# Four groups of value rows summed on TensorE, and the forgetting heads' scores made in pairs, in an encoder block whose last part gathers rows

## The chip, the cores and the metric

One core of a Trainium2 chip runs the whole program. The metric is the device time in microseconds, the median of the runs. It has five engines with a queue each, run in program order and tied by semaphores: TensorE (matmuls), VectorE, ScalarE, GpSimd (which here issues the gathers) and SyncE (which issues the plain loads); and 16 DMA engines that all transfers share.

## The reference, cut to what matters

The block works on 512 tokens of 1024 numbers (4 tiles of 128 tokens). It has an attention part and a PEER part:

```python
h = h + mixed @ w_out                 # mixed: 8 forgetting heads and 4 differential heads
hn = _rmsnorm(h, norm2_g)
# PEER, for each token and each of 8 heads: two top-16 searches over 128 key scores,
# a top 16 over the 16x16 sums, then
u_sel = jnp.take(u_tab, eidx, axis=0)          # 16 rows of 1024 from 16384
hid = gelu(einsum('thkd,td->thk', u_sel, xb)) * g
v_sel = jnp.take(v_tab, eidx, axis=0)          # 16 rows of 1024
h = h + einsum('thk,thkd->td', hid, v_sel)
out = _rmsnorm(h, final_g)
```

All of it is float32. The scores of a forgetting head are q times k, with 64 numbers contracted, plus a bias from the running sum of the log forget gates, for keys up to the token's tile: 128, 256, 384 or 512 columns for tiles 0 to 3.

## The kernel before, in words

**The order of the work.** Tile 0 is taken through attention first (`BEFORE`). Then its PEER heads start while tiles 1 to 3 are still to go through attention. Seven PEER heads of tile 0 (`HOST_HEADS`) host that other work: this is the hosted loop. The remaining 25 head turns (one of tile 0, eight of each other tile) follow in the tail, in which a gather brings a `u` row and a `v` row in one go (`peer_uv`, 8 KB per token), VectorE makes the dot products, ScalarE a diagonal of the coefficients, and TensorE sums the `v` rows in two banks (`peer_group`, L994).

**The hosted loop.** A head has 16 rows per token, taken in 4 groups (`GRP`) of 4 (`COLS`), so there are 28 slots, one for each group. A slot has nine gaps. In gaps 0, 2, 4 and 6 VectorE makes a dot product of the slot's own group (`dot`, L1541), in gaps 1, 3, 5 and 7 it adds one value row of the group two slots earlier (`BEHIND = 2`): `h[tile 0] += coef * v_row` (`add_row`, L1577, one 128x1024 instruction). The coefficients (`coefs`, L1567) come in gap 1 from a gelu that ScalarE makes in gap 4 of the slot before. In between stand the pieces of the next head's top-k search. What is called T0 later is the end of the last addition of a group.

**The pieces.** What is left of tiles 1 to 3 is cut into pieces. Each has a cost (`share`), and the pieces are laid over the first 27 slots in proportion to their cumulated cost:

```python
for p in later:
    k = int(at / total * (SLOTS - 1) * GAPS)
    ...
    AFTER[k].append(p)
    at += share(p)
```

`total` is 551.2. Every engine runs the pieces of a gap in that order. The kinds are: `project` (a slab of the input weights: 8 matmuls of 384 columns at L786, or of 256 at L778 for values), `attend` (one step, below), `mix`, `mixT`, `outproj` (4 matmuls of 512 columns, L860, added into `h` by VectorE, L1414), `hT`, `query` and `keys`.

**An attend step.** The forgetting heads of tiles 1, 2 and 3 are steps 0 to 23 of one run (8 heads for each tile). In step s TensorE makes the scores of head s (q times k at L929, the bias at L933, both on the same half of the rows: partitions 0 to 63 for even heads, 64 to 127 for odd ones), then transposes the probabilities of head s - 3 (L950) and multiplies those of head s - 4 with the values (L972). Scores go to a ring of three banks (`sc_b`). VectorE's part of step s takes the scores through the mask with a running minimum (L1442); ScalarE takes the exponential (L1195) and the copy of the transpose (L1188). At step 27 (the last head's values) VectorE scales the mixed values (L1450, L1453). The differential heads follow as steps of their own, with two maps in each, matmuls of the two row halves side by side.

**The product banks.** Each piece that ends in a bank has a number in the list `MM`; it uses bank number modulo 3 of `mm0`, `mm1`, `acc0`, and TensorE waits until the piece three earlier has been emptied (`mm_bank`).

**The rings.** `u_ring` and `v_ring` hold four rows each. GpSimd issues alternately the gather of a `u` row four ahead (L685) and of a `v` row (L692):

```python
def gather_v(n, c):
    if n or c >= V_RING:
        pool.wait_ge(added, TOPK * n + c + 1 - V_RING)
```

so the `v` row c of a group can only be fetched when the row c of the group before has been added.

## Time and profile before

| | |
|---|---|
| median of 3 runs | 1542.28 us (1540.99 to 1546.88) |
| profiled execution, its own time | 1541.62 us |
| its span in the trace | 1539.8 us |
| TensorE busy | 1269.3 us (82%) |
| VectorE busy | 1077.6 us (70%) |
| ScalarE busy | 459.8 us (30%) |
| GpSimd busy | 751.5 us (49%) |
| DMA | 596.50 MB, mean 387 GB/s |
| mean granted TensorE clock | 0.939 |

The busy shares are means over stages with different limits, so they are to be read by stretch: in the rows of the next section but one, each stretch has the busy time of the engines in it, the granted clock and the DMA engines' busy share. A busy TensorE counts overlapping matmuls once; each float32 matmul appears as two rows (passes). The L numbers are lines of the kernel printed above.

### The profile page before, as it was taken

Reading aid. Unit: us, or ns where it says so; the run is one execution under the profiler, and the core shown is the slowest. Engines: PE = TensorE matmul, PEld = TensorE weight load, DVE = VectorE, ACT = ScalarE, POOL = GpSimd, SP = SyncE. Lnnn points to the kernel's source line nnn. Section 1 sums busy time; section 2 is a strip of 40 time slices with the busy share of each in tenths; the row PEclk is TensorE's granted clock in tenths of the full one; section 3 lists DMA queues with packets and bytes.
Section 4 is the critical chain, followed back from the end, with each engine's and each line's share of the span. In section 5 each row is a group of like instructions: output and inputs, shape, how many; then the busy total and the mean of one; then the engine's idle time right before and its main releaser. Section 6 shows DMA issues by size and latency. Waiting matters only on the chain.

```text
span 1539.8 us, 13062 instructions
## 1 busy us (share of the span) xinstructions
PE 1269.3 (82%) x3727; PEld 658.2 (43%) x3727; DVE 1077.6 (70%) x2520; ACT 459.8 (30%) x1200; POOL 751.5 (49%) x637
## 2 busy tenths in 40 slices
PE   9999999988888488999787777677886787777778
PEld 7766655665545234444333333233332233332333
DVE  3247699999988867566666676666666766666654
ACT  3432355466343022222222222221222222222212
POOL 0016477675667443454544554445444554444440
PEclk9999999999989699999899999989999999999998
DMA  9669799997999999999999999999999999999995
GB/s 382 250 250 413 275 330 351 370 376 268 340 371 392 391 421 416 421 421 421 421 422 422 421 422 421 421 422 421 422 421 421 422 422 421 422 420 422 421 421 208
DMA packets 99741, 596.50 MB, mean 387 GB/s; under 512 B 11480, under 2 KB 11480, under 8 KB 42328
## 3 DMA queue, kind: packets, MB, share of 16 engines
q0 software_dynamic: 89856, 536.91, 86.0%
q1 hardware_dynamic: 9816, 58.77, 9.6%
q8 instruction: 31, 0.51, 0.1%
q14 instruction: 38, 0.31, 0.0%
HBM read 593.54 MB, written 2.10 MB: 387 GB/s over the span
## 4 chain that ended last, share of the span: by engine, by line
DMA 42%; PE 15%; DVE 6%; POOL 3%; issue 2%; ACT 2%; DVEq 0%; POOLq 0%
PE acc L994 13%; DMA map_mem<-in_peer_uv_dram,eidx 10%; DMA w_ring<-in_peer_uv_dram,eidx 9%; DMA v_all<-in_peer_uv_dram,eidx 7%; DMA act_mem<-in_peer_uv_dram,eidx 6%; DMA v_ring<-in_peer_uv_dram,eidx 3%; DMA mix_mem<-in_peer_uv_dram,eidx 3%; DMA u_ring<-in_peer_uv_dram,eidx 3%; DMA v_ring<-in_peer_v_dram,eidx 2%; PE mm L786 1%; ACT diag L1228 1%; DVE map_mem L1549 1%; DVE w_ring L1549 1%; PE sc L786 1%; POOL v_ring L692 1%
## 5 line engine op out<-in xcount | busy, mean ns | idle before, releaser
L1220 ACT ACTIVATE gel<-hid 128x4 f32<-128x4 f32 x126 | 25.8, 205 | 722.2 <-DVE hid L1549 712.5
L685 POOL DMA_INDIRECT u_ring<-in_peer_u_dram,eidx x112 | 136.8, 1221 | 172.9 <-DVE eidx L1529 99.5
L994 PE MATMUL acc<-v_all,diag 128*128 128x512 f32 x256 | 129.2, 651 | 61.1 <-ACT diag L1228 60.6
L692 POOL DMA_INDIRECT v_ring<-in_peer_v_dram,eidx x112 | 133.4, 1192 | 66.4 <-DVE h L1577 38.0
L1577 DVE SCALAR_TENSOR_TENSOR h<-v_ring,coef,h 128x1024 f32<-128x1024 f32 x112 | 143.9, 1284 | 14.3 <-DMA v_ring<-in_peer_v_dram,eidx 11.3
L994 PE MATMUL acc<-map_mem,diag 128*128 128x512 f32 x248 | 123.3, 644 | 32.0 <-ACT diag L1228 32.0
L994 PE MATMUL acc<-v_ring,diag 128*128 128x512 f32 x248 | 120.1, 629 | 32.3 <-ACT diag L1228 28.7
L1541 DVE CUSTOM_DVE_ANT_0 u_ring<-u_ring,hn 128x1024 f32<-128x1024 f32 x112 | 136.6, 1220 | 14.2 <-DMA u_ring<-in_peer_u_dram,eidx 14.0
L994 PE MATMUL acc<-u_ring,diag 128*128 128x512 f32 x248 | 119.1, 626 | 27.4 <-ACT diag L1228 25.8
L1228 ACT ACTIVATE diag<-ident,coef 128x128 f32<-128x128 f32 x392 | 126.3, 390 | 39.1 <-DVE coef L1567 30.8
L711 POOL DMA_INDIRECT v_all<-in_peer_uv_dram,eidx x64 | 76.1, 1189 | 92.3 <-PE acc L994 81.7
L711 POOL DMA_INDIRECT map_mem<-in_peer_uv_dram,eidx x62 | 73.8, 1190 | 95.1 <-PE acc L994 87.0
L711 POOL DMA_INDIRECT v_ring<-in_peer_uv_dram,eidx x62 | 77.2, 1246 | 79.0 <-PE acc L994 68.2
L994 PE MATMUL acc<-w_ring,diag 128*128 128x512 f32 x176 | 89.2, 655 | 24.5 <-ACT diag L1228 24.4
L1549 DVE CUSTOM_DVE_ANT_0 v_all<-v_all,hn 128x1024 f32<-128x1024 f32 x62 | 75.4, 1225 | 47.9 <-DMA v_all<-in_peer_uv_dram,eidx 47.9
L994 PEld LDWEIGHTS acc<-v_all,diag 128*128 128x128 f32 x256 | 51.9, 209 | 132.0 <-issue 132.0
L786 PE MATMUL mm<-act_mem,w_ring 128*128 128x384 f32 x304 | 104.0, 497 | 3.0 <-ACT act_mem L1118 3.0
L1549 DVE CUSTOM_DVE_ANT_0 map_mem<-map_mem,hn 128x1024 f32<-128x1024 f32 x62 | 75.3, 1224 | 43.5 <-DMA map_mem<-in_peer_uv_dram,eidx 43.5
L994 PE MATMUL acc<-act_mem,diag 128*128 128x512 f32 x176 | 86.0, 634 | 23.3 <-ACT diag L1228 23.3
L711 POOL DMA_INDIRECT u_ring<-in_peer_uv_dram,eidx x62 | 72.0, 1161 | 66.7 <-PE acc L994 59.4
L1549 DVE CUSTOM_DVE_ANT_0 v_ring<-v_ring,hn 128x1024 f32<-128x1024 f32 x60 | 72.9, 1226 | 44.1 <-DMA v_ring<-in_peer_uv_dram,eidx 44.1
L1549 DVE CUSTOM_DVE_ANT_0 u_ring<-u_ring,hn 128x1024 f32<-128x1024 f32 x60 | 72.8, 1224 | 41.4 <-DMA u_ring<-in_peer_uv_dram,eidx 41.4
(281 smaller groups left out, 2331.9 us busy)
## 6 DMA issues: line engine op xcount, KB each, us to landing
w_ring<-in_slabs_dram SPq DMA_DIRECT2D x29, 1024.0 KB, 8.4
v_ring<-in_slabs_dram SPq DMA_DIRECT2D x6, 1024.0 KB, 11.2
u_ring<-in_slabs_dram SPq DMA_DIRECT2D x6, 1024.0 KB, 10.9
map_mem<-in_slabs_dram SPq DMA_DIRECT2D x6, 1024.0 KB, 7.9
h<-in_x_dram SPq DMA_DIRECT2D x4, 512.0 KB, 12.5
u_ring<-in_peer_u_dram,eidx POOLq DMA_INDIRECT x112, 6.9
v_ring<-in_peer_v_dram,eidx POOLq DMA_INDIRECT x112, 7.1
v_all<-in_x_cols_dram SPq DMA_DIRECT2D x3, 512.0 KB, 7.4
```

The costliest lines, as they stand in the source:

```text
L685: nc.gpsimd.indirect_dma_start(out=u_ring[:, c % U_RING, :], out_offset=None, in_=peer_u[0], in_offset=bass.IndirectOffsetOnAxis(ap=eidx[n ...
L692: nc.gpsimd.indirect_dma_start(out=v_ring[:, c % V_RING, :], out_offset=None, in_=peer_v[0], in_offset=bass.IndirectOffsetOnAxis(ap=eidx[n ...
L711: nc.gpsimd.indirect_dma_start(out=row_mem[place], out_offset=None, in_=peer_uv, in_offset=bass.IndirectOffsetOnAxis(ap=eidx[n % 3][:, c:c ...
L786: last = nc.tensor.matmul(bk[:, 0:n], w[:, c, q * P:(q + 1) * P], actT[:, c, 0:n], start=(c == 0), stop=(c == KC - 1))
L994: last = nc.tensor.matmul(acc[half][:, :], diag[:, c % COLS, :], v_row(n, c)[:, half * BANK:(half + 1) * BANK], start=first, stop=(n % PH ...
L1220: nc.scalar.activation(gel[:, par, g0:g0 + COLS], hid[:, par, g0:g0 + COLS], ACT.Gelu).then_inc(gelu_done, 1)
L1228: nc.scalar.activation(diag[:, c, :], ident[:, :], ACT.Copy, scale=coef[:, par, g0 + c:g0 + c + 1]).then_inc(diag_done, 1)
L1541: nc.vector.tensor_tensor_reduce(out=u_ring[:, c % U_RING, :], in0=u_ring[:, c % U_RING, :], in1=hn[:, :], scale=1.0, scalar=0.0, op0=ALU. ...
L1549: nc.vector.tensor_tensor_reduce(out=u_row(n, c), in0=u_row(n, c), in1=hn[:, :], scale=1.0, scalar=0.0, op0=ALU.mult, op1=ALU.add, accum_o ...
L1577: nc.vector.scalar_tensor_tensor(out=ht, in0=v_ring[:, c % V_RING, :], scalar=coef[:, par, c:c + 1], in1=ht, op0=ALU.mult, op1=ALU.add).th ...
```

## The change

Two things are changed.

1. The value rows of four groups of tile 0 (5, 9, 13 and 17, of 28) are no longer added by VectorE. A new piece `sum` stands in gap 0 of slot k + 2, ahead of the other pieces of the slot, with a share of 10 each in the placement (the total becomes 591.2, so the pieces behind move by a few gaps). In it ScalarE makes four diagonals of the coefficients (128x128), and TensorE multiplies the four rows with them, in two halves of 512 columns, into two of the three product banks. VectorE adds the two banks into `h` in gap 1 of the next slot (or ahead of an `outproj` that comes first). The coefficients of such a group are made in gap 0 instead of gap 1. A `v` place is given back when TensorE has read it. The diagonals lie in memory that `z_f` and `e_f` used on 8 partitions.
2. The scores of the forgetting heads are made for two heads at a time: in every even step the two products q times k, then the two biases; odd steps make none.

In the diff the places come in this order: the placement, the list of banks, the give-back of rows, GpSimd's gather, TensorE's piece and its scores, ScalarE's piece, VectorE's piece, its addition of the sums, and its hosted loop.

```diff
 BEHIND = 2
+SUMMED = (5, 9, 13, 17)
+SHARE_SUM = 10.0
...
     total, at = sum(share(p) for p in later), 0.0
+    total += SHARE_SUM * len(SUMMED)
+    summed_at = {(k + BEHIND) * GAPS: ("sum", k) for k in SUMMED}
     for p in later:
         k = int(at / total * (SLOTS - 1) * GAPS)
+        while summed_at and k >= min(summed_at):
+            slot = min(summed_at)
+            AFTER[slot].append(summed_at.pop(slot))
+            at += SHARE_SUM
+            k = int(at / total * (SLOTS - 1) * GAPS)
...
+        elif kind == "sum":
+            MM += [(*p, half) for half in range(2)]
...
+        def row_taken(i):
+            if i // COLS in SUMMED and i % COLS == COLS - 1:
+                return mm_full, mm_done(("sum", i // COLS, 1))
+            return added, i + 1 - sum(COLS * k + COLS - 1 <= i for k in SUMMED)
...
             def gather_v(n, c):
                 if n or c >= V_RING:
-                    pool.wait_ge(added, TOPK * n + c + 1 - V_RING)
+                    pool.wait_ge(*row_taken(TOPK * n + c - V_RING))
...
                     last.then_inc(mm_full, 1)
+                elif kind == "sum":
+                    k, = p
+                    pe.wait_ge(*row_taken(COLS * k - 1))
+                    banks = [mm_bank((kind, k, half)) for half in range(2)]
+                    for c in range(COLS):
+                        pe.wait_ge(v_in[c % V_RING], 16 * (k * COLS // V_RING + 1))
+                        pe.wait_ge(sum_diag_done, COLS * SUMMED.index(k) + c + 1)
+                        for half in range(2):
+                            last = nc.tensor.matmul(banks[half][:, :], sum_diag[:, c, :], v_ring[:, c % V_RING, half * BANK:(half + 1) * BANK],
+                                                    start=(c == 0), stop=(c == COLS - 1))
+                            if c == COLS - 1:
+                                last.then_inc(mm_full, 1)
+                        if c < COLS - 1:
+                            last.then_inc(added, 1)
...
+            def pair_scores(g, step):
+                t, first = at_step(g, 0, step)
+                nk, j = P * (t + 1), GROUPS[g].index(t)
+                if first == 0:
+                    pe.wait_ge(selq_ready, 2 * (t + 1))
+                both = [(HD * (m % 2), m // 2, map_no[(t, m)]) for m in (first, first + 1)]
+                for lo, ch, k in both:
+                    if k >= len(sc_b):
+                        pe.wait_ge(sc_drained, k + 1 - len(sc_b))
+                    nc.tensor.matmul(sc_b[k % len(sc_b)][:, 0:nk], qT[lo:lo + HD, ch, j * P:(j + 1) * P], kv_t[lo:lo + HD, ch, 0:nk],
+                                     start=True, stop=False)
+                for lo, ch, k in both:
+                    nc.tensor.matmul(sc_b[k % len(sc_b)][:, 0:nk], selq[lo:lo + 40, ch, t % 2, :], caug[lo:lo + 40, 0:nk],
+                                     start=False, stop=True).then_inc(sc_full, 1)
+
             def scores(g, half, step):
-                if at_step(g, half, step):
+                if half == 0:
+                    if step % 2 == 0 and at_step(g, half, step):
+                        pair_scores(g, step)
+                elif at_step(g, half, step):
...
                                              scale=rstd2[:, t:t + 1]).then_inc(mm_copied, 1)
+                elif kind == "sum":
+                    n, par, g0 = group_at(p[0])
+                    act.wait_ge(coef_done, p[0] + 1)
...
+                    for c in range(COLS):
+                        nc.scalar.activation(sum_diag[:, c, :], ident[:, :], ACT.Copy,
+                                             scale=coef[:, par, g0 + c:g0 + c + 1]).then_inc(sum_diag_done, 1)
...
                 elif kind == "outproj":
                     g, sl, t = p
+                    if sums_due:
+                        add_sum(sums_due.pop())
...
+            def add_sum(k):
+                for half in range(2):
+                    bk = mm_wait(("sum", k, half))
+                    hs = h[:, 0, half * BANK:(half + 1) * BANK]
+                    nc.vector.tensor_tensor(out=hs, in0=bk[:, :], in1=hs, op=ALU.add).then_inc(mm_drained, 1)
...
                     behind = group_at(k - BEHIND)
                     for gap in range(GAPS):
                         c = gap // 2
+                        if gap == 0 and k - BEHIND in SUMMED:
+                            coefs(*behind)
+                            sums_due.append(k - BEHIND)
+                        if gap == 1 and k - BEHIND - 1 in SUMMED and sums_due:
+                            add_sum(sums_due.pop())
...
-                        elif gap < GAPS - 1 and k >= BEHIND:
+                        elif gap < GAPS - 1 and k >= BEHIND and k - BEHIND not in SUMMED:
```

Three more waits on `added` (of the combined gathers, of `eidx` and of the last part) and the wait in `add_row` are written with `row_taken` in the same way; ahead of a row that follows a summed group, `add_row` waits until the banks of the sum have been added.

## Rows read from the trace of the kernel before

**Rows 1.** Stretches: us, busy us (instructions) of PE, PEld, DVE, ACT, POOL; clock, DMA share, GB/s

```profile
225.00:265.00 40.00, 38.67 (x151) 23.41 (x150) 39.62 (x89) 21.96 (x46) 29.45 (x25) 0.96 0.96 357
265.00:327.00 62.00, 61.29 (x286) 43.02 (x285) 59.27 (x113) 28.29 (x55) 45.51 (x38) 1.00 0.98 370
327.00:400.00 73.00, 62.38 (x318) 42.44 (x318) 70.57 (x159) 50.66 (x135) 49.78 (x41) 0.91 0.88 320
400.00:490.00 90.00, 77.67 (x245) 43.34 (x244) 81.79 (x160) 25.12 (x63) 62.14 (x53) 0.92 0.95 362
500.00:800.00 300.00, 247.76 (x606) 115.86 (x607) 204.32 (x486) 73.32 (x194) 142.06 (x124) 0.91 1.01 417
```

**Rows 2.** Timeline of VectorE: start us, duration us, instruction, idle before it

```profile
214.02 1.27 DVE L1577 SCALAR_TENSOR_TENSOR h<-v_ring,coef,h 128x1024 f32<-128x1024 f32 x1
215.56 1.21 DVE L1541 CUSTOM_DVE_ANT_0 u_ring<-u_ring,hn 128x1024 f32<-128x1024 f32 x1
...
266.54 1.31 DVE L1577 SCALAR_TENSOR_TENSOR h<-v_ring,coef,h 128x1024 f32<-128x1024 f32 x1
...
269.22 1.28 DVE L1577 SCALAR_TENSOR_TENSOR h<-v_ring,coef,h 128x1024 f32<-128x1024 f32 x1
270.42 0.68 DVE L1442 CUSTOM_DVE_ANT_0 map_mem<-sc,act_mem 128x512 f32<-128x512 f32 x1
...
318.37 1.31 DVE L1577 SCALAR_TENSOR_TENSOR h<-v_ring,coef,h 128x1024 f32<-128x1024 f32 x1
...
379.94 1.27 DVE L1577 SCALAR_TENSOR_TENSOR h<-v_ring,coef,h 128x1024 f32<-128x1024 f32 x1
...
391.42 0.68 DVE L1414 TENSOR_TENSOR h<-mm,h 128x512 f32<-128x512 f32 x1
...
454.49 0.22 DVE L1567 SCALAR_TENSOR_TENSOR coef<-gel,gate_inv,gexp 128x4 f32<-128x4 f32 x1 [4.83 <-ACT gel L1220]
```

**Rows 3.** Timeline of TensorE, neighbouring passes of one kind merged

```profile
194.52 0.48 PE L929 MATMUL sc<-store 64*128 64x256 f32 x1 [0.47 <-ACT v_all L1082]
194.53 0.48 PE L929 MATMUL acc<-store 64*128 64x256 f32 x1
...
195.49 0.59 PE L929 MATMUL sc<-store 64*128 64x256 f32 x2
...
208.28 0.70 PE L929 MATMUL acc<-store 64*128 64x256 f32 x2
...
209.34 0.44 PE L950 MATMUL tr<-ident,map_mem 128*128 128x128 f32 x2
...
267.55 1.12 PE L929 MATMUL sc<-store 64*128 64x512 f32 x2
...
269.47 0.55 PE L950 MATMUL tr<-ident,map_mem 128*128 128x128 f32 x3
...
323.04 3.67 PE L778 MATMUL acc<-w_ring,act_mem 128*128 128x256 f32 x16
326.55 1.00 PE L972 MATMUL o<-v_all,map_mem 128*128 128x64 f32 x8
...
368.47 2.07 PE L929 MATMUL acc<-store 64*128 64x512 f32 x2 [5.34 <-DVE negmax L1442]
```

**Rows 4.** Groups of ScalarE by line and shape: busy us, mean ns

```profile
L1228 ACT ACTIVATE diag<-ident,coef 128x128 f32<-128x128 f32 x392 | 126.3, 390 | 39.1 <-DVE coef L1567 30.8 <-PE acc L994 8.3
```

**Rows 5.** The chain that ended last, in the tail: start us, us

```profile
596.87 13.73 PE acc L994 x32
```

**Rows 6.** Timeline of GpSimd, its gathers of value rows

```profile
216.41 1.18 POOL L692 DMA_INDIRECT v_ring<-in_peer_v_dram,eidx  x1 [0.31 <-issue]
...
270.10 1.21 POOL L692 DMA_INDIRECT v_ring<-in_peer_v_dram,eidx  x1 [0.30 <-issue]
...
323.45 1.68 POOL L692 DMA_INDIRECT v_ring<-in_peer_v_dram,eidx  x1 [0.30 <-issue]
```

**Rows 7.** The tile v_ring, 200 to 450 us: issue to landing

```profile
DMA to landing us min/median/max: 4.7/6.6/10.0
```

More of the change, by code:

```diff
@@ L387, in build @@
         c_all = sb("c_all", [FH, SEQ])
[L388 to L389 removed]
+        gate_mem = sb("gate_mem", [P, 2 * max_n])
+        z_f = gate_mem[0:FH, 0:max_n]
+        e_f = gate_mem[0:FH, max_n:2 * max_n]
+        sum_diag = gate_mem[:, 0:COLS * P].rearrange("p (a n) -> p a n", a=COLS)
         selq = mix_mem[:, D:D + FH * P].rearrange("p (a b n) -> p a b n", a=FH // 2, b=2)
@@ L923, in scores @@
                             pe.wait_ge(sc_drained, k + 1 - len(sc_b))
-                        bk = sc_b[k % len(sc_b)]
-                        if m < FH:
-                            lo, ch = HD * (m % 2), m // 2
-                        else:
-                            lo, ch = HD * ((m - FH) % 2), KC // 2 + (m - FH) // 2
-                        mo = nc.tensor.matmul(bk[:, 0:nk], qT[lo:lo + HD, ch, j * P:(j + 1) * P], kv_t[lo:lo + HD, ch, 0:nk],
-                                              start=True, stop=(m >= FH))
-                        if m < FH:
-                            mo = nc.tensor.matmul(bk[:, 0:nk], selq[lo:lo + 40, m // 2, t % 2, :], caug[lo:lo + 40, 0:nk], start=False, stop=True)
-                        mo.then_inc(sc_full, 1)
+                        lo, ch = HD * ((m - FH) % 2), KC // 2 + (m - FH) // 2
+                        nc.tensor.matmul(sc_b[k % len(sc_b)][:, 0:nk], qT[lo:lo + HD, ch, j * P:(j + 1) * P], kv_t[lo:lo + HD, ch, 0:nk],
+                                         start=True, stop=True).then_inc(sc_full, 1)
             def turned_map(g, half, step):
@@ L1573, in add_row @@
                 dve.wait_ge(coef_done, GRP * n + c // COLS + 1)
-                if n or c:
-                    dve.wait_ge(added, TOPK * n + c)
+                before = (TOPK * n + c - 1) // COLS
+                if c % COLS == 0 and before in SUMMED:
+                    dve.wait_ge(*emptied(("sum", before, 1)))
+                elif n or c:
+                    dve.wait_ge(*row_taken(TOPK * n + c - 1))
                 ht = h[:, n // PH, :]
```

14 lines of the change are left out of this document (7 added, 7 removed).

## The prediction, made before the change was run

> **What bounds the kernel now.** I read the stretch table first [rows 1]. From 500 us on the 16 DMA engines are full (share 1.01, 417 GB/s), and nothing after that frees them. From there the bytes that are left decide, and one microsecond lost or won before that point arrives at the end about one to one. What can move it is the hosted loop (28 slots of 9 gaps, about 110 to 490 us), in which VectorE works through tile 0's rows with the pieces of tiles 1 to 3 between them. There VectorE is busy 39.6 of 40 us (225 to 265 us) and 59.3 of 62 us (265 to 327 us), TensorE 38.7 and 61.3 of the same, and the DMA share is 0.96 and 0.98. So three engines are all near full up to 327 us; later TensorE (62.4 of 73 us) and DMA (0.88) have room and VectorE (70.6 of 73 us) hasn't.
>
> Then the timelines, to see who leads. TensorE finishes the scores of head step 17 (the second one of 512 columns) at 269.47, and VectorE takes them at 270.42 [rows 2, 3]. TensorE's lead is 1 us there, and VectorE doesn't wait: they are just in time. A stop of TensorE longer than its lead becomes a stop of VectorE.
>
> **VectorE's share of the change.** 16 row additions go. One lasts 1.28 us, and 1.20 us from its start to the next instruction's (269.22 to 270.42) [rows 2]: 16 x 1.20 = 19.2 us. Eight 128x512 additions from PSUM come, 0.68 us each (391.42) and, by the same overlap of 0.08, 0.6 us of the chain [rows 2]: 8 x 0.6 = 4.8 us. Net -14.4 us, 3.6 per group. ScalarE gets 16 diagonals of 0.39 us [rows 4], 6.2 us, hidden: it is busy 50.7 of 73 us at most [rows 1]. If they weren't hidden they'd stand inside the sums' wait for rows below, since four of them (1.6 us) are over before the last row lands.
>
> **TensorE's share.** A sum is 4 rows by 2 halves, 8 matmuls of 512 columns. The chain shows 32 passes of that kind in 13.73 us, two passes to a matmul: 0.86 us each [rows 5]. 8 x 0.86 = 6.9 us per sum, 27.5 us for four. The paired scores give some back. A head at 256 columns takes 1.06 us on its own (208.28 to 209.34), yet two heads whose matmuls happened to stand together went at 194.52 to 195.5, both banks at once, 0.97 us for two [rows 3]. The second of the rows at 194.5 starts 0.01 us after the first, so row halves do run side by side and the saving is real: about 1.1 us per pair at 256 columns. At 512 a head is 1.92 us (267.55 to 269.47) [rows 3] and a pair, at the 0.43 us of a 512-column pass four times and a start of 0.1, about 1.8: saving 2.0. At 384 columns, between the two, a head is 1.5 and a pair 1.4: saving 1.6. Four pairs per tile: 4 x (1.1 + 1.6 + 2.0) = 18.8 us, less one pair at 256 that is already together: 17.7 us. TensorE's work grows by 9.8 us net. The Trainium skill says in TensorEngine Tiling (Array Packing), Key Properties, that different row tiles can execute in parallel but that changing the tiling mode drains the engine; by the first half the pairing wins what the rows say, by the second a part of it would go at each switch between 128-row and 64-row work, and the switches are in both kernels, fewer in the new one.
>
> **The wait that comes with the sum.** TensorE works in program order, and the sum stands in gap 0 of slot k + 2, ahead of that slot's steps. It has to wait (a) for the last addition of group k - 1, call its end T0, and (b) for row c = 3 of its own group. That row's gather may start only when the same ring place is free, at T0, because group k - 1's last row held it. Now VectorE asks for it a whole slot later and it's there; in the new order TensorE asks at once. GpSimd is near full too: it issues it at 216.41 for group 5 (T0 = 215.3, the end of the addition at 214.02), 270.10 for group 9 (267.9) and 323.45 for group 13 (319.7) [rows 2, 6], so 1.1, 2.2 and 3.8 us late; for group 17 (381.2) I take the 1.1. From issue to landing takes 4.7 to 10.0, median 6.6 us [rows 7]. The last two matmuls take 1.7 us. The sum ends at T0 + 9.4, 10.5, 12.1 and 9.4 us.
>
> Next who is late. By the placement rule (a piece's cumulated share over the total, 551.2 before and 591.2 after, times 243 gaps) I placed the pieces of both kernels. After each sum stands something that VectorE needs in the same slot:
> - group 5, slot 7: steps 9 (gap 5) and 10 (gap 6). TensorE adds 0.8 us of transposes and values and 1.4 of the pair: ready at T0 + 11.7. VectorE, with four dots of 1.2 us [rows 2], coefficients of 0.3 and two strips of 0.5, is there at T0 + 6.1. Wait 5.6.
> - group 9, slot 11: step 18 (gap 5), the pair at 512 columns, 1.8 us: ready T0 + 12.5. VectorE after three dots: T0 + 3.9. Wait 8.6.
> - group 13, slot 15: step 27 (gap 8) needs the last values; before them stand step 26 (1.3), a value projection (3.5, from 323.04 to 326.55) and step 27's own 0.9 [rows 3]: ready T0 + 17.8, VectorE there at T0 + 5.1. Wait 12 to 13, I take 12. In the old order these values are done by 327.5, T0 + 7.8.
> - group 17, slot 19: mixT, then differential step 11 (gap 5): 0.45 + 1.8 + 1.1: ready T0 + 12.9, VectorE at T0 + 3.9. Wait 9.0.
>
> Sum of waits 35.2 us. Then the banks: a sum holds two of three product banks until gap 1 of the next slot. Only after group 17 does this bite: the two output projections of slot 20, gaps 1 and 2, can't begin before the banks are emptied; each is 4 matmuls, 3.4 us, against about 2.1 and 1.8 us of other VectorE work: 1.3 + 1.6 = 2.9 us.
>
> **Credits.** VectorE's wait of 4.83 us at slot 24 for a gelu behind a query copy [rows 2] shrinks, since that query now stands behind the gelu; it's partly taken up a slot later: 3. Tile 0's pairs at 128 columns, where TensorE leads the start: 0 to 2.4, I take 1.5.
>
> **Sum.** -14.4 + 35.2 + 2.9 - 4.5 = +19.2 us. The profiled execution took 1541.6 us by its own count (span 1539.8), 0.7 below the median of 1542.3, so I add to it, 1560.8, and say 1560.
>
> **Unknown costs, from both sides.** Landing of the last row: 4.7 to 10.0 us instead of 6.6, so -7.6 to +13.6 over four. GpSimd's lag: 1.1 to 3.8 us, -4 to +7. The pair at 384 and 512 columns, which no row shows: between the one at 256 columns scaled by columns (1.5 and 1.9 us) and no overlap at all (3.0 and 3.8 us), in which case TensorE is the bound from 225 to 327 us and 12 us more are due. The clock: after a wait of 5.34 us the two passes at 368.47 took 2.07 us where 1.12 (267.55) is usual [rows 3]: twice as long, as at the lower of its two clock levels (1.2 for 2.4 GHz); the stretch from 327 to 400 us, where this happened, has a mean granted clock of 0.91 [rows 1]. If each sum's wait has this effect, what follows it costs 1 to 3 us more each, 4 to 12 in all. The Trainium skill's page TensorE: Matmul & The Clock Gate (Why this matters for your kernels) warns of idle gaps between bursts; by the trace it does happen after such waits, but inside a sum the rows come one by one, so I count nothing for it in the sum.
>
> **Rivals.**
> - *The additions' saving passes on (faster).* If the last row lands early and the paired scores have put TensorE ahead, VectorE is not stopped and 14.4 us come out of its chain. What decides is the wait per sum: below 3.6 us each it is a gain. For it: rows can land in 4.7 us, and odd steps need no scores. Against: even 1.1 + 4.7 + 1.7 us is T0 + 7.5, ahead of which no step of the slot can be scored. DMA caps it as well: 0.96, 0.98, 0.88 and 0.95 of four stretches [rows 1] leave about 16 us in all but 1.2 between 265 and 327 us. Time 1528 to 1534.
> - *Break-even.* Waits of 4 to 6 us a sum, as group 5's: four times 5.6 is 22.4, with 2.9 - 14.4 - 4.5: +6.4, time 1548; with fast landings (1.9 each) 1540.
> - *TensorE becomes the bound.* The stalls and low clock together, or no overlap of the pairs: +30 to +40, 1572 to 1582.
> - *Nothing reaches the end* because the DMA tail absorbs it: against it stands that the tail is full from 500 us [rows 1], with no idle to give.
>
> **How the numbers follow.** Stalls as worked out 0.50, TensorE as the bound 0.10, break-even 0.20, saving passes on 0.18, tail absorbs 0.02. A difference below 0.5% (7.7 us, 1534.6 to 1550.0) is about what a measurement of this kernel can't tell from none. The likeliest has 1552 to 1573 by itself; with break-even and part of the gain on one side and part of the bound case on the other, 1532 to 1578. Faster 0.20, same 0.20, slower 0.60.
>
> **What would show it.** In the new profile: TensorE waiting 4 to 8 us at the sum's line on v_ring landings, four times; VectorE's strip line waiting for the score matmuls at about 225, 280, 335 and 400 us, the third longest (at the mix of slot 15); slot 20's output additions waiting for their matmul; score rows of two banks that start within 0.02 us of each other; the full-rate DMA stretch beginning some 15 to 20 us later. I am wrong if VectorE stays above 95% busy through slots 7, 11, 15 and 19, or if TensorE's lead at a sum turns out to be many microseconds because pairs are done long before VectorE wants them.

## The result, and the profile after

The changed kernel takes 1582.43 us (1579.78 to 1584.19), the kernel before 1542.01 beside it: ratio 1.0254, 95% interval 1.0228 to 1.0281, 40 us slower. I had said 1560 us (1532 to 1578): the side is right, the time lies 4 us above the range. The profiled span is 1578.0 us, 38.2 longer.

The stretch table of the changed kernel (us, busy us of the five engines, clock, DMA share, GB/s), first four rows beside [rows 1]:

```profile
225.00:265.00 40.00, 38.13 (x176) 23.68 (x175) 35.43 (x82) 18.99 (x41) 25.48 (x23) 1.00 0.91 328
265.00:327.00 62.00, 51.64 (x237) 35.20 (x237) 49.96 (x103) 28.40 (x54) 41.54 (x35) 0.92 0.91 329
327.00:400.00 73.00, 56.50 (x246) 36.06 (x245) 54.76 (x132) 38.51 (x99) 36.13 (x34) 0.88 0.78 267
400.00:505.00 105.00, 83.03 (x294) 46.91 (x295) 79.42 (x164) 39.15 (x100) 60.13 (x53) 0.89 0.85 302
540.00:600.00 60.00, 35.32 (x79) 16.61 (x80) 42.96 (x100) 12.92 (x34) 31.00 (x27) 0.77 0.99 403
```

TensorE, VectorE and GpSimd are less busy than before from 265 us on, and ScalarE has room throughout, so none of them is the bound over the whole loop: they wait for each other. The DMA share is 0.78 where it was 0.88, and 0.99 again from 540 us. The last dot product of the loop starts at 540.0 (before 501.5) and 1038.0 us remain to the end of the span (before 1038.3). So what the loop loses arrives at the end one to one.

What VectorE lost, from the first dot of slot 5 to the loop's last dot. Its busy time there (third engine column), before and after:

```profile
189.40:501.50 312.10, 276.29 (x1142) 175.83 (x1140) 291.85 (x594) 148.51 (x350) 220.75 (x183) 0.93 0.94 349
```

```profile
190.50:540.00 349.50, 288.07 (x1193) 178.46 (x1191) 277.61 (x586) 155.02 (x365) 208.23 (x181) 0.93 0.87 311
```

and its waits in the same stretches (who waited for whom: us in total, times, longest), before:

```profile
DVE h L1577 <- DMA v_ring<-in_peer_v_dram,eidx: 5.4, 4, 2.2
DVE coef L1567 <- ACT gel L1220: 4.8, 1, 4.8
DVE u_ring L1541 <- DMA u_ring<-in_peer_u_dram,eidx: 2.1, 4, 0.8
DVE rinv L1402 <- ACT stat L1064: 0.8, 3, 0.3
```

and after:

```profile
DVE map_mem L1496 <- PE sc L976: 12.1, 2, 11.2
DVE u_ring L1595 <- DMA u_ring<-in_peer_u_dram,eidx: 10.6, 7, 3.6
DVE rinv L1504 <- PE o L1015: 9.0, 1, 9.0
DVE coef L1621 <- ACT gel L1271: 8.9, 2, 4.9
DVE map_mem L1496 <- PE acc L961: 7.4, 1, 7.4
DVE h L1468 <- PE mm L894: 5.6, 3, 3.6
DVE map_mem L1496 <- PE sc L961: 4.2, 1, 4.2
DVE rinv L1454 <- ACT stat L1107: 2.8, 3, 1.3
DVE stat L1452 <- ACT xs L1101: 2.3, 2, 1.3
DVE h L1468 <- PE acc L894: 1.4, 2, 0.9
DVE h L1634 <- DMA v_ring<-in_peer_v_dram,eidx: 0.7, 2, 0.4
```

VectorE has 14.2 us less work, as forecast, and its waits grow from 16.8 to 69.1 us (all rows of both views, some not shown): +52.3. The interval is 37.4 us longer. Four waits of 4.2, 7.4, 9.0 and 11.2 us stand exactly where the prediction put them, behind the four sums. They are 31.8 of the 52.3 us. The other 20 are waits that I had forecast as small, as nothing or as a gain.

Where the time goes is seen from the first dot of each slot. The table has how much longer each slot lasts than in the kernel before (us), in the changed kernel and in the kernel "shift only" of the experiments, which has the moved pieces and no sum:

| slots | changed kernel | shift only |
|---|---|---|
| 7, 11, 15, 19 (a sum in each) | 0.5, 3.5, 4.3, 7.2: together 15.5 | -2.3, -1.4, -3.4, -0.3: together -7.4 |
| 16, 17, 18, 21, 22 | 4.4, 1.7, 1.4, 1.0, 2.5: together 11.0 | 5.1, 1.7, 1.3, 1.8, 3.5: together 13.4 |
| 20 | 6.2 | -0.4 |
| all others from 5 on | 4.7 | 0.2 |

Why a sum ends late is read on TensorE and ScalarE. Group 17 on TensorE (16 passes merged; then the output projections of slot 20):

```profile
405.23 9.28 PE L867 MATMUL mm<-v_ring,gate_mem 128*128 128x512 f32 x16 [6.39 <-ACT gate_mem L1205]
...
426.29 8.99 PE L894 MATMUL mm<-w_ring,store 128*128 128x512 f32 x16 [7.63 <-DVE h L1642]
```

and ScalarE just before:

```profile
400.67 1.28 ACT L1246 ACT_TABLE_LOAD   x1
401.96 0.72 ACT L1246 ACTIVATE map_mem<-map_mem,negmax 128x512 f32<-128x512 f32 x1
...
403.52 0.40 ACT L1256 ACTIVATE xs<-ident,rowsum 128x128 f32<-128x128 f32 x1
...
404.70 1.26 ACT L1205 ACTIVATE gate_mem<-ident,coef 128x128 f32<-128x128 f32 x4
```

TensorE is released not by a row but by the first diagonal. ScalarE makes the diagonals in its own order, behind a table load, the exponentials of the step before and their follow-up. TensorE is idle for 6.39 us, and then 16 passes take 9.28 us, where the 32 passes of [rows 5] at 13.73 make 6.9. The other sums, of groups 5, 9 and 13, on TensorE:

```profile
220.33 1.10 PE L867 MATMUL mm<-v_ring,gate_mem 128*128 128x512 f32 x2 [3.07 <-ACT gate_mem L1205]
...
226.02 1.13 PE L867 MATMUL mm<-v_ring,gate_mem 128*128 128x512 f32 x2 [0.30 <-DMA v_ring<-in_peer_v_dram,eidx]
...
273.81 2.04 PE L867 MATMUL acc<-v_ring,gate_mem 128*128 128x512 f32 x2 [8.28 <-ACT gate_mem L1205]
...
333.16 8.80 PE L867 MATMUL mm<-v_ring,gate_mem 128*128 128x512 f32 x16 [2.72 <-ACT gate_mem L1205]
```

They begin with an idle time of 3.07, 8.28 and 2.72 us that the first diagonal ends; for rows the matmuls wait 0.30 us in all. In group 9 two passes take 2.04 and 1.9 us until 279 us (granted clock 0.50 from 273.8 to 279.0 us), then 1.02: the lower and the upper clock level (1.2 and 2.4 GHz), after 8.28 us without work. The Trainium skill (TensorE: Matmul & The Clock Gate, Why this matters for your kernels) warns of idle gaps between bursts; this trace agrees for groups 9, 13 and 17, and not for group 5, whose passes were at full clock.

That the rows are hardly waited for doesn't mean that they came early. GpSimd issued the last row of each of the four groups here:

```profile
216.94 0.94 POOL L712 DMA_INDIRECT v_ring<-in_peer_v_dram,eidx  x1 [0.30 <-issue]
...
274.11 0.94 POOL L712 DMA_INDIRECT v_ring<-in_peer_v_dram,eidx  x1 [0.30 <-issue]
...
332.22 0.94 POOL L712 DMA_INDIRECT v_ring<-in_peer_v_dram,eidx  x1 [0.30 <-issue]
...
403.37 1.81 POOL L712 DMA_INDIRECT v_ring<-in_peer_v_dram,eidx  x1 [0.59 <-DVE h L1634]
```

In group 5 the last row released the last four passes at 226.02, 10.3 us after T0 (215.7). For the others an estimate, with the median landing of 6.6 us [rows 7] and 1.7 us for the last two matmuls: by their rows alone these sums could have ended at 282.4, 340.5 and 411.7 us, and they ended at 283.9, 342.0 and 414.5. So diagonals and last rows were late nearly together in three of the four.

### The profile page after: what moved, and what is told of

Same layout as the page of the kernel before. It is cut to its first block, busy times and chain, and to the rows that moved or that the text cites. A ratio compares the mean times of both kernels' runs of the same rounds, so it can differ in the third digit from the quotient of the medians.

```text
span 1578.0 us, 13210 instructions
## 1 busy us (share of the span) xinstructions
PE 1280.4 (81%) x3791; PEld 661.1 (42%) x3791; DVE 1062.9 (67%) x2512; ACT 469.3 (30%) x1221; POOL 746.7 (47%) x637
## 4 chain that ended last, share of the span: by engine, by line
DMA 41%; PE 18%; DVE 6%; ACT 2%; POOL 2%; issue 2%; another core or an unknown queue 0%; DVEq 0%; POOLq 0%; ACTq 0%
PE acc L1037 12%; DMA map_mem<-in_peer_uv_dram,eidx 10%; DMA v_all<-in_peer_uv_dram,eidx 7%; DMA w_ring<-in_peer_uv_dram,eidx 7%; DMA act_mem<-in_peer_uv_dram,eidx 6%; DMA mix_mem<-in_peer_uv_dram,eidx 4%; PE mm L806 3%; DMA u_ring<-in_peer_uv_dram,eidx 3%; DMA v_ring<-in_peer_uv_dram,eidx 3%; ACT diag L1279 1%; DVE map_mem L1603 1%; DMA v_ring<-in_peer_v_dram,eidx 1%; DVE w_ring L1603 1%; PE acc L806 1%; DVE h L1634 1%
## 5 line engine op out<-in xcount | busy, mean ns | idle before, releaser
L705 POOL DMA_INDIRECT u_ring<-in_peer_u_dram,eidx x112 | 131.6, 1175 | 205.3 <-DVE eidx L1583 97.8
L712 POOL DMA_INDIRECT v_ring<-in_peer_v_dram,eidx x112 | 129.2, 1153 | 83.2 <-DVE h L1634 48.9
L1634 DVE SCALAR_TENSOR_TENSOR h<-v_ring,coef,h 128x1024 f32<-128x1024 f32 x96 | 123.4, 1286 | 10.4 <-DMA v_ring<-in_peer_v_dram,eidx 5.2
L806 PE MATMUL mm<-act_mem,w_ring 128*128 128x384 f32 x320 | 109.4, 498 | 7.6 <-ACT act_mem L1161 4.9
L1037 PEld LDWEIGHTS acc<-v_all,diag 128*128 128x128 f32 x256 | 52.3, 210 | 129.3 <-issue 129.3
## 6 DMA issues: line engine op xcount, KB each, us to landing
u_ring<-in_slabs_dram SPq DMA_DIRECT2D x6, 1024.0 KB, 10.6
```

What stands on the lines that cost most here:

```text
L705: nc.gpsimd.indirect_dma_start(out=u_ring[:, c % U_RING, :], out_offset=None, in_=peer_u[0], in_offset=bass.IndirectOffsetOnAxis(ap=eidx[n ...
L712: nc.gpsimd.indirect_dma_start(out=v_ring[:, c % V_RING, :], out_offset=None, in_=peer_v[0], in_offset=bass.IndirectOffsetOnAxis(ap=eidx[n ...
L806: last = nc.tensor.matmul(bk[:, 0:n], w[:, c, q * P:(q + 1) * P], actT[:, c, 0:n], start=(c == 0), stop=(c == KC - 1))
L1037: last = nc.tensor.matmul(acc[half][:, :], diag[:, c % COLS, :], v_row(n, c)[:, half * BANK:(half + 1) * BANK], start=first, stop=(n % PH ...
L1634: nc.vector.scalar_tensor_tensor(out=ht, in0=v_ring[:, c % V_RING, :], scalar=coef[:, par, c:c + 1], in1=ht, op0=ALU.mult, op1=ALU.add).th ...
```

## The experiments

Each ratio is to the kernel before, run beside it. The median of the kernel before went from 1541.4 to 1545.0 us beside these runs, so where two of these runs weren't run side by side, a difference of 3 us or less says nothing. "Changed kernel" stands for 1582.4 us. Diffs are against it unless said otherwise, and "..." stands for lines left out.

### The parts alone

**Pairs only.**

```diff
-SUMMED = (5, 9, 13, 17)
+SUMMED = ()
```

> The changed kernel without any summed group (no sums, no shift of the pieces), only the forgetting heads' scores in pairs. Stall theory: the pairs cost nothing and the slowdown comes from the sums. The changed kernel's first dot product came 2.9 us earlier, so 1536 to 1541 us, against 1542 before. Rival (the pairs hurt, since a pair needs two of three score banks at once): above 1548 us.

1544.87 us, ratio 1.0017 (1.0006 to 1.0027): no gain. Its waits for scores (L961) are 4.4 us where 2.6 stood before. TensorE's saving comes out in part as idle time (3.03 us before 319.94, for the next map), and at the mix of slot 15 VectorE waits 4.0 us.

**Sums only.** Scores head by head, as before:

```diff
-            def pair_scores(g, step):
...
             def scores(g, half, step):
-                if half == 0:
-                    if step % 2 == 0 and at_step(g, half, step):
-                        pair_scores(g, step)
...
```

> The changed kernel with the four sums and the shifted pieces, but the scores one head at a time as before. Stall theory: TensorE is stopped at each sum anyway, so its lost 17.7 us of pairing show only in part: 1586 to 1596 us (4 to 14 us over the changed kernel). Rival (TensorE's load is the bound from 225 to 327 us): all of it shows, 1598 to 1602 us.

1591.15 us, ratio 1.0318 (1.0290 to 1.0347). The pairs give back 8.7 us when the sums have made TensorE late, and nothing when they haven't.

**Shift only.** The kernel before, its pieces placed as if four sums of 10 shares were there:

```diff
+    total += 10.0 * 4
+    summed_at = {(k + BEHIND) * GAPS: k for k in (5, 9, 13, 17)}
     for p in later:
         k = int(at / total * (SLOTS - 1) * GAPS)
+        while summed_at and k >= min(summed_at):
+            summed_at.pop(min(summed_at))
+            at += 10.0
+            k = int(at / total * (SLOTS - 1) * GAPS)
```

> The kernel before with nothing but the shifted placement of the pieces: the four shares of 10 are counted in, no sum stands there, all rows are added by VectorE, scores one by one. Stall theory: the earlier place of the forget piece costs some 4 us by slot 7 and the rest little, 1542 to 1550 us. Rival (the shift, which crowds the pieces between the summed slots, makes most of the 40 us): 1560 us or more.

1553.59 us, ratio 1.0071 (1.0045 to 1.0097): 12 us for a move that I had costed at nothing. Between both expectations. By the table above it loses 13.4 us in five slots that hold no sum, and gains 7.4 in the four that the pieces moved out of; by its last dot it is 10.0 us late, 4.1 of them before slot 5.

### What a sum waits for

**Resident rows.** The sums read the resident `g2b` and not `v_ring`, so they don't wait for rows; GpSimd waits for a row's landing before it fetches into the same place. The output leaves those 64 rows out.

```diff
...
-                        pe.wait_ge(v_in[c % V_RING], 16 * (k * COLS // V_RING + 1))
+                        pe.wait_ge(gains_in, 16)
...
-                            last = nc.tensor.matmul(banks[half][:, :], sum_diag[:, c, :], v_ring[:, c % V_RING, half * BANK:(half + 1) * BANK],
+                            last = nc.tensor.matmul(banks[half][:, :], sum_diag[:, c, :], g2b[:, half * BANK:(half + 1) * BANK],
```

> The changed kernel, but the sums multiply the diagonals with a tile that lies in memory (the norm gains) instead of the gathered rows, so that TensorE does not wait for a landing; the rows are still fetched, and GpSimd waits for their landing itself before it fetches into the same place. The output leaves these 64 rows out. Stall theory, by the wait for the last row: each sum ends 2 to 4 us earlier, 1566 to 1575 us. Rival (the waits are for the diagonals and the low clock, or it is TensorE's load): 1578 to 1584 us.

1581.96 us, ratio 1.0259 (1.0233 to 1.0284): no gain, so the rows are not what holds the sums as long as the diagonals come late. Every sum still waits for its diagonals:

```profile
PE mm L869 <- ACT gate_mem L1207: 10.7, 3, 4.9
PE acc L869 <- ACT gate_mem L1207: 6.4, 1, 6.4
```

The run isn't a clean one. In group 5 the same idle time as in the changed kernel is followed by passes at the lower clock, where there they were at the upper one:

```profile
220.73 2.04 PE L869 MATMUL mm<-g2b,gate_mem 128*128 128x512 f32 x2 [3.07 <-ACT gate_mem L1207]
```

Slot 7 loses 2.9 us for it, not 0.5, while slots 11, 15 and 19 together lose 2.2 us less.

**No inputs waited for.** Besides, the identity in the place of the diagonals: only T0, the last addition of the group before, is waited for. The output leaves the 64 rows out. Against the kernel with resident rows:

```diff
-                        pe.wait_ge(sum_diag_done, COLS * SUMMED.index(k) + c + 1)
...
-                            last = nc.tensor.matmul(banks[half][:, :], sum_diag[:, c, :], g2b[:, half * BANK:(half + 1) * BANK],
+                            last = nc.tensor.matmul(banks[half][:, :], ident[:, :], g2b[:, half * BANK:(half + 1) * BANK],
```

> The changed kernel whose sums multiply the identity with resident data, so that they wait neither for rows nor for diagonals, only for the last addition of the group before; the output leaves the 64 rows out. Theory (VectorE's last addition, the diagonals and the clock make the stop together): each sum starts about 3 us earlier, but partly at the low clock: 1568 to 1578 us. If the diagonals are the whole stop: 1560 us or less. If only the load counts: 1580 us.

1570.48 us, ratio 1.0172 (1.0138 to 1.0206): 12 us of the 40 are the waits for diagonals and rows together. How they are shared between the two isn't shown: no run has early diagonals and gathered rows at this place.

**Filled wait.** Four matmuls of resident data into the sum's bank ahead of its wait, to keep TensorE at work (the wait for the banks moves ahead with them):

```diff
+                    banks = [mm_bank((kind, k, half)) for half in range(2)]
+                    pe.wait_ge(gains_in, 16)
+                    for _ in range(4):
+                        nc.tensor.matmul(banks[0][:, :], ident[:, :], g2b[:, 0:BANK], start=True, stop=True)
                     pe.wait_ge(*row_taken(COLS * k - 1))
-                    banks = [mm_bank((kind, k, half)) for half in range(2)]
```

> The changed kernel with four more 512-column matmuls (3.4 us at full clock) on resident data ahead of each sum's first wait, so that less of the wait is idle. If the low clock behind the wait is a main part of the cost, each sum after a long wait (9, 13, 17) ends 1 to 3 us earlier: 1572 to 1578 us. If it is only the waits and the load: 1582 to 1590 us, later where the wait is shorter than the filler.

1580.0 us, ratio 1.0246 (1.0209 to 1.0283): its interval overlaps that of the changed kernel, so no gain is shown. The sums' passes fall from 715 to 612 ns in the banks `mm`, near the 592 of full clock. So TensorE kept at work keeps its clock, but the clock isn't where most of the time goes.

### Cut into pieces

**Row by row.** A sum is four pieces of two matmuls at gaps 1, 3, 5 and 7, 2.5 shares each; T0 and the banks are waited for with the first, and ScalarE makes all four diagonals there:

```diff
-    summed_at = {(k + BEHIND) * GAPS: ("sum", k) for k in SUMMED}
+    summed_at = {(k + BEHIND) * GAPS + 2 * c + 1: ("sumrow", k, c) for k in SUMMED for c in range(COLS)}
...
-            at += SHARE_SUM
+            at += SHARE_SUM / COLS
...
```

> The changed kernel with each sum cut into four pieces, one for each row, in gaps 1, 3, 5 and 7 of the slot (a share of 2.5 each), so that TensorE does not stand still at one point until the last addition of the group before, the diagonals and the last row are there. Theory (TensorE's stop at the sum, made of the wait for VectorE and ScalarE and of the low clock behind it, is the cost; the shift of the pieces another 12 us): the stops nearly go, 1545 to 1558 us. Rival (TensorE's 27.5 us of added matmuls are the cost): 1572 us or more.

1571.27 us, ratio 1.0181 (1.0143 to 1.0220). Eleven better than the changed kernel, 28 worse than before.

**The same, half the share** (`SHARE_SUM = 5.0`).

> As the row by row kernel, with a share of 5 for a sum instead of 10, so that the pieces are shifted half as far (the forget piece stands in gap 0 of slot 4, behind only one gap's work less than before). If the shift costs what the shift alone showed (12 us for 10), 4 to 8 us less than the kernel with a share of 10; if the crowding was needed to make room for the sums, the same or more.

1568.29 us, ratio 1.0161 (1.0127 to 1.0194): 3 us less, not 4 to 8, and the intervals of the two overlap, so that even this isn't shown.

**Row by row, no inputs waited for** (both edits above; the output leaves the 64 rows out).

> The row-by-row kernel (four pieces of two matmuls to each sum), but the matmuls read resident data and the identity, so that a sum waits for the last addition of the group before (T0) and for nothing else; VectorE does the same work as in the changed kernel. The output leaves the 64 summed rows out. It has TensorE's load, the shift of the pieces and VectorE's saving, and hardly a wait. If the waits (diagonals, rows) are what is left of row-by-row's +28 us, the time falls to 1548 to 1558 us: the shift's +12 less a part of VectorE's 14. If TensorE's added load, coming where it is full, is what is left, it stays at 1562 to 1570 us.

1562.23 us, ratio 1.0111 (1.0090 to 1.0131): without a wait for an input, 18 us are still lost. VectorE's largest waits are 14.7 us for `u` rows and 9.4 us for the values ahead of the mix. Slots 16, 17, 18, 21 and 22, where the shift alone loses, have 11.1 us of the loss.

### One sum

**Group 5 alone**, with its share (`SUMMED = (5,)`).

> Paired scores and one sum only, that of group 5, with its share of 10 in the placement. By the terms of my prediction a sum of group 5 costs a wait of 5.6 us and saves VectorE 3.6: +2, so on top of the paired scores alone (1544.9) 1546 to 1549 us. If a sum costs a quarter of what the four cost together on top of the pairs (+37), as it would when the shift and TensorE's load come with each, 1552 to 1556 us.

1553.54 us, ratio 1.0062 (1.0046 to 1.0079): 8.7 above the pairs alone (6.9 by the ratios), where my terms say 2. Slot 7 loses 5.2 us, and the five slots of the shift 7.7.

**Group 17 alone, unshifted** (`SUMMED = (17,)`, `SHARE_SUM = 0.0`).

> Paired scores and one sum only, that of group 17, with a share of 0, so that no other piece moves. By the terms of my prediction it costs a wait of 9.0 us and 2.9 us for the two output projections of slot 20, and saves 3.6: +8.3 us on the paired scores alone (1544.9), 1550 to 1555 us. If the shift is the larger part of a sum's cost, little is left without it: 1545 to 1549 us.

1562.36 us, ratio 1.0119 (1.0103 to 1.0135): one sum costs 17.5 us (15.7 by the ratios), about twice my 8.3, and no piece is shifted. The waits of VectorE from 380 to 430 us:

```profile
DVE map_mem L1496 <- PE sc L976: 11.9, 1, 11.9
DVE h L1468 <- PE mm L894: 6.6, 2, 5.0
DVE rinv L1454 <- ACT stat L1107: 1.5, 2, 1.3
DVE stat L1452 <- ACT xs L1101: 1.4, 1, 1.4
```

11.9 for my 9.0 and 6.6 for my 2.9 (the two output projections stand at the end of slot 19 here), and the mix's chain through ScalarE (2.9), which was hidden before (0.8 us, row above), stands open after VectorE's stop. 21.4 less the 3.6 saved makes 17.8.

### Another place, and the diagonals ahead

**The four sums at gap 6.**

```diff
-    summed_at = {(k + BEHIND) * GAPS: ("sum", k) for k in SUMMED}
+    summed_at = {(k + BEHIND) * GAPS + 6: ("sum", k) for k in SUMMED}
```

> The changed kernel with its four sums put at gap 6 of their slots and not at gap 0: the diagonals and rows are there by then, and the scores that VectorE needs at gap 5 stand ahead of the sum. If the place ahead of the slot's steps is what costs, most of the waits of 7.4 and 11.2 us in the slots of groups 9 and 17 and TensorE's idle time before the sums go: 1553 to 1565 us. If TensorE's load is what costs wherever it stands, the wait moves to the next slot: 1572 to 1584 us.

1573.4 us, ratio 1.0198 (1.0180 to 1.0216). It is 9 us faster than the changed kernel. The waits move from the scores to the sum itself:

```profile
DVE h L1642 <- PE mm L867: 15.8, 5, 9.0
DVE u_ring L1595 <- DMA u_ring<-in_peer_u_dram,eidx: 13.8, 10, 3.5
```

and TensorE is still idle 15.2 us ahead of the sums, for the diagonals: they moved with the piece in ScalarE's order too.

**Group 17 alone at gap 4** (`+ 4` in that line, `SUMMED = (17,)`, share 0).

> One sum (group 17, share 0, paired scores) at gap 4 of its slot and not at gap 0. The transposes and values of that slot's first gaps go ahead of it, so that TensorE has work while the diagonals are made, but the differential scores of gap 5 still stand behind it. At gap 0 it took 1562.4 us, with waits of 11.9 and 6.6 us. If the idle time of 5.1 us before the sum and the low clock after it count: 1553 to 1558 us. If only the 7 us of load ahead of the scores count: 1559 to 1563 us.

1555.31 us, ratio 1.0093 (1.0076 to 1.0110). On TensorE:

```profile
392.62 2.04 PE L867 MATMUL mm<-v_ring,gate_mem 128*128 128x512 f32 x2 [8.16 <-ACT gate_mem L1205]
```

**The four sums at gap 6, diagonals at gap 0.** On ScalarE a piece `sumdiag` of its own; the other engines pass over it (on top of the edit that puts the sums at gap 6):

```diff
+    for k in SUMMED:
+        AFTER[(k + BEHIND) * GAPS].insert(0, ("sumdiag", k))
...
-                elif kind == "sum":
+                elif kind == "sumdiag":
                     n, par, g0 = group_at(p[0])
                     act.wait_ge(coef_done, p[0] + 1)
...
```

> The four sums at gap 6 on TensorE, their diagonals at gap 0 on ScalarE. With both at gap 6 it took 1573.4 us, with 15.2 us of TensorE idle before the sums and 20.8 us of VectorE waiting for them. If the late diagonals are what holds it, both shrink by 10 or more: 1558 to 1566 us. If TensorE's load is, the time stays: 1569 to 1575 us. Faster than the kernel before (1542) only if a sum cost TensorE nothing.

1558.89 us, ratio 1.0111 (1.0087 to 1.0136). One piece moved in one engine's order brings 14.5 us. No sum waits for a diagonal any more (for rows 0.6 us), and all run at full clock:

```profile
L869 PE MATMUL mm<-v_ring,gate_mem 128*128 128x512 f32 x40 | 19.7, 599 | 1.0 <-DMA v_ring<-in_peer_v_dram,eidx 0.6 <-issue 0.5
L869 PE MATMUL acc<-v_ring,gate_mem 128*128 128x512 f32 x24 | 12.3, 592 | 0.0
```

Most of the 16 us that are left stand where no sum does: slots 16, 17, 18, 21 and 22 lose 12.8 us, as with the shift alone (13.4). At the sums, slots 7 and 8 lose 4.4 us together, and slots 11, 15 and 19 are 7.1 us shorter than before.

**Group 17 alone at gap 4, diagonals at gap 0.**

> One sum (group 17, share 0, paired scores) at gap 4 on TensorE, its diagonals at gap 0 on ScalarE. With both at gap 4 it took 1555.3 us, with an idle time of 8.2 us before the sum and a wait of 8.9 us of VectorE for it; the paired scores alone take 1544.9. If the diagonals hold it: 1544 to 1551 us. If the load does: 1553 to 1557 us.

1545.57 us, ratio 1.0018 (1.0004 to 1.0033). The sum that cost 17.5 us now costs 0.7 on the pairs alone, which is none that can be told. The sum at its start, and its last row:

```profile
381.87 1.10 PE L869 MATMUL mm<-v_ring,gate_mem 128*128 128x512 f32 x2 [0.49 <-ACT gate_mem L1207]
...
387.82 1.13 PE L869 MATMUL mm<-v_ring,gate_mem 128*128 128x512 f32 x2 [0.56 <-DMA v_ring<-in_peer_v_dram,eidx]
```

With the diagonals early, it is the last row that ends the last wait: 6.9 us after T0 (380.9), and the sum is over at T0 + 8.9. The prediction had T0 + 9.4 for this sum, by this row.

**Four sums at gap 5, diagonals at gap 0, share 0.**

> Four sums at gap 5, diagonals at gap 0, share 0, so that no other piece moves; paired scores. If the shift is what is left of the cost of 1558.9 us, it falls by 8 to 14: 1545 to 1551 us. If TensorE's load between 225 and 327 us is, it stays at 1555 to 1562 us.

1565.12 us, ratio 1.0129 (1.0113 to 1.0146): a miss: slower, not faster, than the kernel with the sums at gap 6. But two things differ between the two, the shift and the gap: at gap 5 a sum stands ahead of the steps of that gap, at gap 6 behind them. Slots 16, 17, 18, 21 and 22 now lose 2.7 us and not 12.8, so the shift's part is gone. By the starts of the slots the loss comes in slots 7 (5.7 us), 12 (7.9), 15 and 16 (9.0) and only 2.6 in slot 19: in the main where TensorE was full before, [rows 1], and less where it had room. 17.7 us are waits for the values ahead of a mix.

**The same with the scores head by head.**

> The same with the scores made head by head, as in the kernel before. The pairing alone cost 3 us, but saved 9 when the sums stood in the changed kernel. If TensorE is full while the sums are there, it is 5 to 10 us slower than with pairs; if the sums fit into TensorE's room, 0 to 3 us faster, 1538 to 1548 us, and it might beat the kernel before (1542).

1565.08 us, ratio 1.0134 (1.0115 to 1.0152): the pairs are worth nothing here. Another miss. Sums at gap 6 with early diagonals and a share of 0 were not run.

**Groups 17 and 21, gap 4, share 0, diagonals at gap 0, scores head by head**, an attempt to beat the kernel before:

> Sums for groups 17 and 21 only, at gap 4 of their slots, diagonals at gap 0 on ScalarE, share 0, scores made head by head as in the kernel before. VectorE saves 2 x 3.6 us and TensorE is 66 to 100% busy there. If a sum is free where TensorE has room and the saving passes on: 1534 to 1539 us, faster than before. If, as in the run with one, the saving is used up by waits for the output projections behind the sum: 1540 to 1546 us.

1553.4 us, ratio 1.0076 (1.0063 to 1.0090). Slots 5 to 19 start within 0.7 us of before, slot 20 starts 2.3 later, slot 25 10.5 later. Group 21's sum stands behind a projection that itself waits 2.96 us for ScalarE, and VectorE waits for the sum:

```profile
447.72 7.89 PE L808 MATMUL mm<-act_mem,w_ring 128*128 128x384 f32 x16 [2.96 <-ACT act_mem L1154]
```

```profile
461.66 0.69 DVE L1635 TENSOR_TENSOR h<-mm,h 128x512 f32<-128x512 f32 x1 [9.67 <-PE mm L869]
```

No version beats the kernel before.

## Why the prediction was partly wrong, by its own steps

**The step that failed** is the one that looked for the cost only behind the sums. By my terms the four slots with a sum lose 16.0 us (waits of 35.2 less 16 additions of 1.20), and all other slots from 5 on 4.7 (eight bank additions, 4.8, and 2.9 for the output projections, less the credit of 3). The trace has 15.5 us in the four slots and 22.0 in the others: 11.0 of them in slots 16, 17, 18, 21 and 22, where the shifted pieces alone lose 13.4, and 6.2 in slot 20. I had placed the shifted pieces, and used their places only to look at the four waits; what the shift does elsewhere was put at nothing but the credit, without a reason.

| term of the sum | forecast | in the trace after |
|---|---|---|
| VectorE's work | -14.4 | -14.2 |
| waits behind sums 5, 9, 13, 17 | 5.6 + 8.6 + 12 + 9.0 = 35.2 | 4.2 + 7.4 + 9.0 + 11.2 = 31.8 |
| output projections behind the banks | 2.9 | 7.0 (5.2 of it in slot 20) |
| gelu waits (slot 24's) | -3 | +4.1 (4.8 in slot 24 before; 4.0 in slot 25 and 4.9 in slot 27 after) |
| tile 0's pairs | -1.5 | not shown: the first dot starts anywhere from 3.7 us earlier to 2.2 later in the kernels with pairs |
| `u` rows late | none | +8.5 |
| `v` rows late | none | -4.7 |
| mix's chain through ScalarE | none | +4.3 |

**VectorE's share: right.** So is that the loop's loss arrives at the end one to one, and that the passes of a pair start together: 0.01 us apart at 384 columns, and at 512 two heads in 1.8 us (283.88 to the last pair's start at 285.28 and its 0.43), as worked out.

**The wait that comes with the sum: the places right, one of its two causes left out.** I let the sum wait for row c = 3, and hid the diagonals inside that wait ("they'd stand inside the sums' wait for rows"). In the changed kernel it is rather the other way round: the first diagonal comes 2.7 to 8.3 us after TensorE is free, and the wait for rows is hidden behind it. The row wait is real, though: taking the rows away changed nothing (1582.0), rows and diagonals together 12 us, and with early diagonals a row was the last to come, 0.5 us from the forecast end of the sum. Early diagonals took 14.5 us off four sums at gap 6 and 9.7 off one at gap 4. The sign that I had named, TensorE waiting 4 to 8 us for rows four times, didn't show. Asking whether ScalarE has room was the wrong question. What decides is what stands ahead of the diagonals in its order. One thing there is a load of 1.28 us for the exponential's table. The Trainium skill (ScalarE: Activation LUTs, What ACT_TABLE_LOAD costs) has 1.283 us for it, and the trace agrees; the drain of about 1.38 us that it adds for each switch doesn't show, since the exponential starts 0.01 us behind the load (400.67 + 1.28, 401.96). Another is VectorE: ahead of group 9's diagonals stands an exponential for which ScalarE itself waits 2.13 us (at 271.75) until VectorE has made a strip. That the four waits add up to nearly my number is in part luck: sums ended at T0 + 11.4 to 12.8 for my 9.4 to 12.1, while VectorE in three of four places came later itself.

**The clock: listed, and left out of the sum.** The argument was that rows come one by one. The four sums take about 7.5, 10.0, 8.8 and 9.3 us, 35.6 in all for my 27.5, and the output projections after group 17 8.99 for 6.9: 10 us of TensorE, within my 4 to 12. As time it is less; filling the wait gave nothing that can be told from none.

**The credits: the wrong sign.** I took a wait away where a query copy stood ahead of a gelu. That wait is gone, but two others for a gelu have come, in slots 25 and 27: 8.9 us for 4.8. And I let VectorE save 3.6 us in each of four slots without asking whether the `u` rows come faster. In those slots three dots follow each other at 1.14 us, and a gather takes GpSimd 1.2 us to issue [rows 6], with a `v` row's between two of them. Waits for `u` rows are 5.3 to 14.7 us in the kernels with four sums, and 2.1 before. In the changed kernel 10.4 of their 10.6 us lie in slots 7, 11 and 15, ahead of VectorE's wait for TensorE, so that there they cost little or nothing by themselves. That the issue rate is the cause is argued; no run isolated it from the time that a row takes to land.

**The shift: costed at one credit, measured at +12 alone.** Its mark is slots 16, 17, 18, 21 and 22: they lose 10.4 to 13.4 us in nine of the ten kernels with four shares of 10 (20.9 in the tenth, with sums and diagonals at gap 6, where a sum's wait falls into slot 16), 7.4 with half the share, and 0.1 to 2.7 in the six with a share of 0. So about 11 of the changed kernel's 40 us go there. In the four slots with a sum the shift alone saves 7.4 us; whether it does so beside the sums stays open.

**TensorE's load.** The rival "TensorE becomes the bound", 1572 to 1582 with a chance of 0.10, has the number, and a part of the cause: stalls and low clock there are, pairs that don't overlap there aren't, and TensorE isn't the bound (busy 51.6 of 62 us from 265 to 327, before 61.3). Of the 40 us, moving the sums to gap 6 takes 9, early diagonals 14.5 more. Of the 16 that are left, hardly with a wait for an input and at full clock, the shift's five slots hold 12.8. That TensorE's order is in it too is suggested, not shown: one sum where TensorE has room costs 0.7 us (group 17), one where it has none makes slot 7 5.2 us longer (group 5, with late diagonals), and four at gap 5 without a shift lose 20 us, most of it in the full slots.

## What to carry to other kernels

When a step is given to another engine, follow each of its inputs back to the place where its producer makes it in its own queue; a small operation on an idle engine, placed behind long ones, stopped one of the fullest engines here. With it ahead, and the sum four gaps later, 17.5 us of cost became 0.7. Work saved on one of three engines that are all near full was worth nothing here, where it landed on the second. When a fixed order is moved to make room, look at every slot and not only at those of the change: the moved pieces alone cost 12 us, in slots without a sum. When several edits are costed together, a credit needs as much proof as a cost: here a credit was a term with the wrong sign.

## What the runs showed of the hardware

- After idle times of 2.72, 6.39 and 7.63 us of TensorE in the changed kernel, and of 5.13 us with group 17's sum alone, 16 passes took 8.8 to 9.3 us, where 6.9 is usual. After 3.07 us (group 5) they didn't slow down: 1.10 us for the first two, 1.02 for the next. In the run with resident rows the same sum began after the same 3.07 us, and its first two passes took 2.04. So the length of the idle time right before a burst doesn't decide alone.
- Four matmuls of resident data in the idle time brought the sums' passes in the banks `mm` from 715 to 612 ns; the time changed by 2.4 us, which can't be told from none.
- Paired passes on the two halves of the rows start 0 to 0.01 us apart at 384 and at 512 columns too. The Trainium skill (TensorEngine Tiling (Array Packing), Key Properties) says that a change of tiling mode drains TensorE. Of a drain no more than 0.1 us is seen here: the sum's last pass, the second of the two at 282.92, starts 0.43 us after the first, and the pair starts at 283.88, 0.53 us after it.
